# GpSimd makes the low half of every seventh weight chunk of the experts

## The chip, the cores and the metric

One core of one Trainium2 chip runs the whole program. The metric is the device time of one execution in microseconds (us). Three runs of the kernel before took 1637.53, 1638.44 and 1640.66 us; the median is 1638.44 us. A profiled execution is a run of its own; all positions below (such as 1096.76) are microseconds from the start of its span.

## The reference, cut to what matters

The model has two layers over 256 tokens of width 1024. The last part of the second layer is a mixture of experts, and this part holds all that the change touches:

```python
def moe_swiglu(x, router, w_gate, w_up, w_down):
    logits = (x @ router).astype(jnp.float32)
    top_vals, top_idx = lax.top_k(logits, TOP_K)          # TOP_K = 2 of N_EXPERTS = 8
    gates = jax.nn.softmax(top_vals, axis=-1)
    combine = jnp.sum(jax.nn.one_hot(top_idx, N_EXPERTS) * gates[..., None], axis=-2)
    y = jnp.zeros_like(x)
    for e in range(N_EXPERTS):
        y = y + combine[..., e:e + 1] * swiglu(x, w_gate[e], w_up[e], w_down[e])
    return y
```

`swiglu` is `(silu(x @ w_gate) * (x @ w_up)) @ w_down`. Per expert `w_gate` and `w_up` are 1024 x 3584 and `w_down` is 3584 x 1024, all float32.

## The kernel before, in words

**Chunks.** All weights stream from HBM in chunks of 128 partitions x 2048 float32 (1 MB). The even and odd layers take 98 chunks (`N0`), each expert 42 (`EC`): 28 for gate and up (four per 512 hidden columns: gate, gate, up, up) and 14 for down. SyncE issues the DMAs in chunk order into a ring of raw buffers, six before the experts and seven in them (`NEXP = 7`; `raw_exp[n % 7]`).

**High and low halves.** A float32 product is made of three products in the type `float32r`. For each chunk ScalarE writes the high half, `w_hi = raw` rounded (a copy, line 1116 in the profile, semaphore `hi_made`). Then VectorE writes the low half, `w_lo = raw - w_hi` (`w_split`, line 1964 in the experts; `split`, line 1483, before them; semaphore `lo_made`). TensorE waits for `lo_made` and runs 12 matmuls per chunk of the experts: for each of 4 rows of weights hi x hi (line 397), hi x lo (398), lo x hi (399). At the end it counts up `chunk_used`.

**Buffers.** There are three pairs of `w_hi`/`w_lo` and, in the experts, a fourth pair `w_hi_more`/`w_lo_more`. The table `E_SLOT` gives each chunk of an expert its pair, in cycles of 4, 4, 4, 4, 4, 3, 3, 4, 4, 4, 4 chunks (`E_CYCLES`). So most chunks use the pair that was used four chunks before, and the chunks 23 to 28 the one used three chunks before. ScalarE can write `w_hi` of a chunk only when that earlier chunk is used.

**One expert.** Each engine runs the same list of 42 steps per expert, in an order written out by hand (`expert(job, z)` on TensorE, ScalarE and VectorE). The first seven experts are a loop, the eighth (`z`) is written out with extra work. At step c VectorE makes the low halves of `E_SPLIT[c]`, that is of chunk c + 4 or c + 3. Besides: at step 0 it makes two `pick` tiles for the next expert (`picks`, line 1855), which TensorE reads in the `index` matmuls (line 793) just before chunk 4 (`C_INDEX = 4`). At steps 3, 7, 11, ... it makes `e_h`, the hidden activations (line 1957), which TensorE transposes (line 864) after chunks 5, 9, 13, ... . `eT_lo` (line 1973) is the low half of these transposed activations.

**GpSimd.** It makes masks, and five low halves before the experts (`split`, line 1010, same subtraction). In the loop over the experts it only issues one indirect DMA per expert (`get_x`, line 1077), which gathers the rows of the next expert. In the eighth expert it issues the gathers of the results of the others (`get_y`, line 1086), each after VectorE has added the one before (`add_got`, line 1932, semaphore `y_added`). In that expert VectorE also computes the row numbers (lines 1890 to 1910) and the gate weights (lines 1915 to 1926).

**What else waits for the low halves.** SyncE issues the DMA of chunk c when the low half of chunk c - 7 is made, since that frees the raw buffer.

Of the kernel before, what the change touches and what calls it, by code (L numbers as in the profile page):

```python
# [18 lines left out]
F32 = mybir.dt.float32  # L19
# [3 lines left out]
ALU = mybir.AluOpType  # L23
# [8 lines left out]
def trunk(nc, x, mem, ln_g, ln_b, mem_wq, mem_wkv, mem_wo, ab_w_in, ab_sinks, ab_w_out,  # L32
# [4 lines left out]
    TB = SEQ // P  # L37
# [11 lines left out]
    W = 512  # L49
# [61 lines left out]
    with ExitStack() as ctx:  # L111
# [172 lines left out]
        for n in range(NSPL + 1, EC + NSPL + 1):  # L284
            at_step = max(at_step, max(m for m in range(-EC, n) if E_SLOT[m % EC] == E_SLOT[n % EC]))
            E_SPLIT[at_step].append(n)
        C_GOT = {12 + 4 * n: (n // TB, n % TB) for n in range(2 * TB)}
# [77 lines left out]
        def _(pe):  # L365
            pair = [0]

            def chunk_product(c, outs, lhs_hi, lhs_lo, k0, first, last, cols, idx=None, slot=None,
                              rows=None, done=None, ready=None, turned=False):
# [3 lines left out]
                pe.wait_ge(lo_made, c + 1 if idx is None else idx + 1)  # L373
# [449 lines left out]
            def expert(job, z):  # L823
                start = list(claims)
                for c in range(EC):
# [14 lines left out]
                    if c < 4 * EJ:  # L840
                        j, q = c // 4, c % 4
                        key, b = (f"{z}eg{j}", j % 2) if q < 2 else (f"{z}eu{j}", 2 + j % 2)
                        if q % 2 == 0:
                            claim(pe, key, b, job, signal=False)
                        chunk_product(c, [(0, bank[b])], xe_hi, xe_lo, 4 * (q % 2), q % 2 == 0,
                                      q % 2 == 1, W, idx=idx, slot=E_SLOT[c], done=chunk_used)
                    else:
# [3 lines left out]
                        if i == 0:  # L851
# [4 lines left out]
                                      done=chunk_used)  # L856
# [29 lines left out]
        def _(sp):  # L886
# [14 lines left out]
            def expert_chunks(e, job, first=False):  # L901
                for c in range(EC):

                    if first and c < NRAW:
                        sp.wait_ge(lo_made, N0 + c - NRAW + 1)
                    elif first and c == NRAW:

                        wait_filled(sp, "router0")
                    else:
                        sp.wait_ge(lo_made, N0 + c - NEXP + 1 + EC * job)  # L910
# [31 lines left out]
        def _(pool):  # L942
# [153 lines left out]
            last = pool.value_load(last_job[0:1, 0:1], min_val=NE - 1, max_val=2 * NE - 1)  # L1096
            with pool.Fori(0, last) as job:
                pool.wait_ge(sem("index_made"), job + 1)
                pool.sem_inc(sem("x_asked"), 1)
                get_x()  # L1100
            for half in range(2):

                pool.wait_ge(sem(f"y_kept{half}"), 16 * last + 16)
                pool.sem_inc(sem("y_asked"), 1)
            pool.wait_ge(sem("rows_made"), 1)
            for g in range(2 * TB):
                get_y(g)

# [345 lines left out]
        def _(dve):  # L1454
# [492 lines left out]
            def expert(job, z):  # L1947
                for c in range(EC):
# [12 lines left out]
                    def w_split(n, job=job):  # L1961
                        r, s = n % NEXP, E_SLOT[n % EC]
                        dve.wait_ge(hi_made, N0 + n + 1 + EC * job)
                        tt(w_lo[s][:, :], raw_exp[r][:, :], w_hi[s][:, :].bitcast(F32),  # L1964
                           ALU.subtract).then_inc(lo_made, 1)
# [89 lines left out]
```

## Time and profile before

| what | value |
|---|---|
| median of three runs | 1638.44 us |
| span of the profiled execution | 1639.8 us |
| TensorE matmul busy | 1599.7 us (98%) |
| VectorE busy | 1259.6 us (77%) |
| ScalarE busy | 1029.8 us (63%) |
| GpSimd busy | 121.1 us (7%) |
| mean granted clock of TensorE | 0.991 |

The page gives the span of the profiled execution from its first to its last instruction and no time of its own beside it. The span is 1.4 us above the median of the three runs. A digit row of the page (one digit for each fortieth of the span, 9 for 90% or more) has TensorE at 9 nearly everywhere, VectorE at 8 or 9 in the last 60%, where the experts are, and the DMA engines at 9 there. In a group of instructions the columns are: line, engine, operation, what it writes and reads, shapes, count, busy time in all, mean duration in ns, and then how long the engine was idle just before these instructions and what ended that.

### The profile page before, as it was taken

The numbers are of one execution on the slowest core, as the hardware profiler recorded it, in microseconds if no ns is written. First come the engines' busy times: TensorE is split into PE (matmuls) and PEld (weight loads), VectorE is DVE, ScalarE is ACT, GpSimd is POOL, SyncE is SP. The second block draws the span as 40 slices with busy tenths as digits, with TensorE's granted clock in tenths as the row PEclk, the third lists the DMA queues.
The fourth block names the chain that finished last, engine by engine and source line by source line (L and its number), as shares of the span: only waits on it lengthen the run. The fifth ranks groups of instructions, "written<-read, shape, count | busy, mean of one in ns | idle before, by whom it ended". The sixth has DMA issues, their size and how long they took to land.

```text
span 1639.8 us, 22497 instructions
## 1 busy us (share of the span) xinstructions
PE 1599.7 (98%) x8202; PEld 1347.1 (82%) x8202; DVE 1259.6 (77%) x1173; ACT 1029.8 (63%) x920; POOL 121.1 (7%) x131
## 2 busy tenths in 40 slices
PE   9999999999999998999999999999999999999996
PEld 8888988888896796888888888888888888888775
DVE  4687475554647656889889889888988988988996
ACT  4564444343437454677777777777777777777673
POOL 2103010000104101000000000000000000000120
PEclk9999999999999999999999999999999999999999
DMA  9437656466455363899999999999999999999992
GB/s 351 164 127 252 213 182 216 128 219 200 161 193 185 135 206 105 318 364 377 389 363 385 389 364 375 389 371 384 388 368 387 388 358 386 388 362 389 359 369 94
DMA packets 238397, 481.24 MB, mean 293 GB/s; under 512 B 8256, under 2 KB 11360, under 8 KB 238336
## 3 DMA queue, kind: packets, MB, share of 16 engines
q1 hardware_dynamic: 229744, 454.06, 77.3%
q0 software_dynamic: 6576, 22.68, 4.1%
q10 hardware_dynamic: 2016, 3.67, 0.6%
q8 instruction: 40, 0.66, 0.2%
q14 instruction: 21, 0.17, 0.0%
HBM read 474.07 MB, written 11.56 MB: 296 GB/s over the span
## 4 chain that ended last, share of the span: by engine, by line
PE 84%; DVE 9%; issue 2%; DMA 2%; ACT 2%; POOL 1%; POOLq 0%; DVEq 0%; SPq 0%; ACTq 0%
PE bank L397 23%; PE bank L399 23%; PE bank L398 23%; PE bank L387 3%; PE bank L390 3%; PE bank L389 3%; DVE w_lo L1483 2%; PE bank L864 1%; DVE w_lo L1964 1%; DMA y_got<-y_rows,row_i 1%; PE bank L684 1%; PE bank L660 1%; DVE X L1520 1%; ACT w_hi L1116 1%; DVE X L1529 1%
## 5 line engine op out<-in xcount | busy, mean ns | idle before, releaser
L1116 ACT ACTIVATE w_hi<-raw 128x2048 fp32r<-128x2048 f32 (+1 forms) x322 | 608.8, 1895 | 258.7 <-PE bank L399 220.3
L1964 DVE TENSOR_TENSOR w_lo<-raw,w_hi 128x2048 fp32r<-128x2048 f32 x221 | 503.1, 2290 | 81.8 <-ACT w_hi L1116 78.5
L1483 DVE TENSOR_TENSOR w_lo<-raw,w_hi 128x2048 fp32r<-128x2048 f32 (+1 forms) x96 | 211.2, 2204 | 145.5 <-ACT w_hi L1116 145.2
L397 PE MATMUL bank<-w_hi,xe_hi 128*128 128x512 f32 x736 | 292.9, 398 | 1.2 <-DVE w_lo L1964 1.2
L399 PE MATMUL bank<-w_hi,xe_lo 128*128 128x512 f32 x736 | 287.9, 391 | 0.0
L398 PE MATMUL bank<-w_lo,xe_hi 128*128 128x512 f32 x736 | 287.4, 390 | 0.0
L399 PEld LDWEIGHTS bank<-w_hi,xe_lo 128*128 128x128 f32 x736 | 138.5, 188 | 29.9
L397 PEld LDWEIGHTS bank<-w_hi,xe_hi 128*128 128x128 f32 x736 | 138.6, 188 | 28.8 <-DVE w_lo L1964 1.6
L398 PEld LDWEIGHTS bank<-w_lo,xe_hi 128*128 128x128 f32 x736 | 138.8, 189 | 27.4
L1964 DVE TENSOR_TENSOR w_lo_more<-raw,w_hi_more 128x2048 fp32r<-128x2048 f32 x63 | 144.2, 2290 | 18.5 <-ACT w_hi_more L1116 11.4
L397 PE MATMUL bank<-w_hi,xT_hi 128*128 128x512 f32 (+1 forms) x384 | 147.0, 383 | 0.1
L399 PE MATMUL bank<-w_hi,xT_lo 128*128 128x512 f32 (+1 forms) x384 | 144.5, 376 | 0.0
L398 PE MATMUL bank<-w_lo,xT_hi 128*128 128x512 f32 (+1 forms) x384 | 144.5, 376 | 0.0
L1116 ACT ACTIVATE w_hi_more<-raw 128x2048 fp32r<-128x2048 f32 x64 | 122.9, 1920 | 28.0 <-PE bank L399 23.8
L397 PE MATMUL bank<-w_hi,eT_hi 128*128 128x512 f32 x320 | 125.8, 393 | 0.5 <-DVE w_lo L1964 0.5
L399 PE MATMUL bank<-w_hi,eT_lo 128*128 128x512 f32 x320 | 124.6, 390 | 0.0
L398 PE MATMUL bank<-w_lo,eT_hi 128*128 128x512 f32 x320 | 124.6, 389 | 0.0
L387 PE MATMUL bank<-xT_hi,w_hi 128*128 128x256 f32 x352 | 101.1, 287 | 2.1 <-DVE w_lo L1483 2.1
L389 PE MATMUL bank<-xT_lo,w_hi 128*128 128x256 f32 x352 | 100.3, 285 | 0.0
L390 PE MATMUL bank<-xT_hi,w_lo 128*128 128x256 f32 x352 | 100.3, 285 | 0.0
L1964 DVE TENSOR_TENSOR w_lo<-raw_more,w_hi 128x2048 fp32r<-128x2048 f32 x40 | 91.4, 2286 | 3.7 <-ACT w_hi L1116 3.7
L1116 ACT ACTIVATE w_hi<-raw_more 128x2048 fp32r<-128x2048 f32 x40 | 76.7, 1916 | 25.0 <-PE bank L399 25.0
(291 smaller groups left out, 2598.4 us busy)
## 6 DMA issues: line engine op xcount, KB each, us to landing
raw<-in_moe_w_gate_dram SPq DMA_DIRECT2D x96, 1024.0 KB, 9.2
raw<-in_moe_w_up_dram SPq DMA_DIRECT2D x96, 1024.0 KB, 8.4
raw<-in_moe_w_down_dram SPq DMA_DIRECT2D x96, 1024.0 KB, 7.2
raw<-in_mem_wkv_dram SPq DMA_DIRECT2D x16, 1024.0 KB, 5.1
raw_more<-in_moe_w_up_dram SPq DMA_DIRECT2D x16, 1024.0 KB, 8.7
raw_more<-in_moe_w_gate_dram SPq DMA_DIRECT2D x16, 1024.0 KB, 8.7
raw_more<-in_moe_w_down_dram SPq DMA_DIRECT2D x16, 1024.0 KB, 7.8
raw<-in_c_w_in_dram SPq DMA_DIRECT2D x12, 1024.0 KB, 5.2
```

Source lines behind the costliest of these rows:

```text
L387: nc.tensor.matmul(d, wh, xh, start=(first and k == 0 and q % 2 == 0), stop=False, skip_group_check=True)
L389: nc.tensor.matmul(d, wh, xl, start=False, stop=False, skip_group_check=True)
L390: m = nc.tensor.matmul(d, wl, xh, start=False, stop=(last and k == n - 1), skip_group_check=True)
L397: nc.tensor.matmul(d, xh, hi[:, k, :], start=(first and k == 0), stop=False)
L398: nc.tensor.matmul(d, xh, lo[:, k, :], start=False, stop=False)
L399: m = nc.tensor.matmul(d, xl, hi[:, k, :], start=False, stop=(last and k == n - 1))
L660: m = nc.tensor.matmul(d[:, t * SEQ:(t + 1) * SEQ], QK[:, 2 * h + k, t * P:(t + 1) * P], MK[:, 2 * h + k, :], start=(k == 0), stop=(k == 1))
L684: m = nc.tensor.matmul(d[:, k * SEQ:(k + 1) * SEQ], MV[:, mb, c:c + P], PT_t[i % 2][:, mb * SEQ:(mb + 1) * SEQ], start=(mb == 0), stop=(mb ...
L864: m = nc.tensor.transpose(d[:, q * P:(q + 1) * P], e_h[j % 2][:, q * P:(q + 1) * P], ident[:, :])
L1116: return nc.scalar.activation(dst, src, ACT.Copy)
L1483: tt(w_lo[s][:, 0:n], raw[c % NRAW][:, 0:n], w_hi[s][:, 0:n].bitcast(F32), ALU.subtract).then_inc(lo_made, 1)
L1964: tt(w_lo[s][:, :], raw_exp[r][:, :], w_hi[s][:, :].bitcast(F32), ALU.subtract).then_inc(lo_made, 1)
```

## The change

Of the 42 chunks of an expert, the six with n % 7 == 5 after the first four, that is 5, 12, 19, 26, 33 and 40, get their low half from GpSimd and not from VectorE. They all lie in the same raw buffer. GpSimd counts them on a semaphore of its own, `lo_by_pool`. `split_done(c, job)` says which semaphore and which value stand for chunk c; TensorE and SyncE wait by it. VectorE leaves these six out. In the loop GpSimd makes chunk 5 ahead of `get_x` and the others behind it. In the eighth expert it makes chunk 5 first, then 12 behind the first pair of gathers, 19 behind the second, and 26, 33 and 40 behind the fourth.

```diff
+        POOL_SPLITS = [n for n in range(NSPL + 1, EC) if n % NEXP == NEXP - 2]
+        DVE_EC = EC - len(POOL_SPLITS)
+
+        def split_done(c, job):
+
+            if c < 0:
+                return split_done(c + EC, job - 1)
+            before_c = sum(n < c for n in POOL_SPLITS)
+            if c in POOL_SPLITS:
+                return sem("lo_by_pool"), before_c + 1 + len(POOL_SPLITS) * job
+            return lo_made, N0 + c + 1 - before_c + DVE_EC * job
...
-                pe.wait_ge(lo_made, c + 1 if idx is None else idx + 1)
+                pe.wait_ge(*((lo_made, c + 1) if idx is None else split_done(c, job)))
...
-                        sp.wait_ge(lo_made, N0 + c - NEXP + 1 + EC * job)
+                        sp.wait_ge(*split_done(c - NEXP, job))
...
+            def w_split(n, job):
+
+                r, s = n % NEXP, E_SLOT[n % EC]
+                pool.wait_ge(hi_made, N0 + n + 1 + EC * job)
+                nc.gpsimd.tensor_tensor(w_lo[s][:, :], raw_exp[r][:, :], w_hi[s][:, :].bitcast(F32),
+                                        ALU.subtract).then_inc(sem("lo_by_pool"), 1)
+
             with pool.Fori(0, last) as job:
+                w_split(POOL_SPLITS[0], job)
                 pool.wait_ge(sem("index_made"), job + 1)
                 pool.sem_inc(sem("x_asked"), 1)
                 get_x()
+                for n in POOL_SPLITS[1:]:
+                    w_split(n, job)
+            w_split(POOL_SPLITS[0], last)
...
+            late_splits = {0: POOL_SPLITS[1:2], 1: POOL_SPLITS[2:3], 2 * TB - 1: POOL_SPLITS[3:]}
             for g in range(2 * TB):
                 get_y(g)
+                for n in late_splits.get(g, ()):
+                    w_split(n, last)
...
                     def w_split(n, job=job):
                         r, s = n % NEXP, E_SLOT[n % EC]
+                        if n in POOL_SPLITS:
+                            return
```

GpSimd's loop over the first seven experts, in the kernel before (`x_got` are the gathered rows, the branch closes the loop):

```order
L1097 UNCONDITIONAL_BRANCH
L1097 ISA
L1077 DMA x_got<-x_rows,got_i 128x1024
L1097 REGISTER_ALU
L1097 COMPARE_AND_BRANCH
L1103 ISA
```

The same loop in the changed kernel (`w_lo_...` and `w_hi_...` are the pairs of buffers, `raw_50` is the one raw buffer of these six chunks):

```order
L1113 TENSOR_TENSOR w_lo_58<-raw_50,w_hi_55 128x2048
L1118 REGISTER_ALU
L1089 DMA x_got<-x_rows,got_i 128x1024
L1112 REGISTER_ALU
L1113 TENSOR_TENSOR w_lo_60<-raw_50,w_hi_57 128x2048
L1112 REGISTER_ALU
L1113 TENSOR_TENSOR w_lo_more<-raw_50,w_hi_more 128x2048
L1112 REGISTER_ALU
L1113 TENSOR_TENSOR w_lo_60<-raw_50,w_hi_57 128x2048
L1112 REGISTER_ALU
L1113 TENSOR_TENSOR w_lo_more<-raw_50,w_hi_more 128x2048
L1112 REGISTER_ALU
```

The loop had one instruction that moves data; now six subtractions stand beside it, one ahead of the gather and five behind. The sixth, of chunk 40, follows the last row shown.

VectorE around the start of an expert (here the eighth, the loop has the same pattern), in the kernel before. The first row is the low half of chunk 4, `w_lo_58<-raw_50` is that of chunk 5, and `raw_more` belongs to chunk 6:

```order
L1964 TENSOR_TENSOR w_lo_60<-raw_49,w_hi_57 128x2048
L1855 ISA
L1855 TENSOR_SCALAR pick<-slot_no,place 128x128
L1855 ISA
L1855 TENSOR_SCALAR pick<-slot_no,place 128x128
L1963 REGISTER_ALU
L1964 TENSOR_TENSOR w_lo_58<-raw_50,w_hi_55 128x2048
L1963 REGISTER_ALU
L1964 TENSOR_TENSOR w_lo_59<-raw_more,w_hi_56 128x2048
```

The same place in the changed kernel:

```order
L1992 TENSOR_TENSOR w_lo_60<-raw_49,w_hi_57 128x2048
L1881 ISA
L1881 TENSOR_SCALAR pick<-slot_no,place 128x128
L1881 ISA
L1881 TENSOR_SCALAR pick<-slot_no,place 128x128
L1991 REGISTER_ALU
L1992 TENSOR_TENSOR w_lo_59<-raw_more,w_hi_56 128x2048
```

The low half of chunk 5 is gone from behind the two picks, and that of chunk 6 moves up. The picks and all ahead of them stay where they were.

## Rows read from the trace of the kernel before

**Rows 1.** Page, part 1: busy time, share of the span, instructions of each engine

```profile
PE 1599.7 (98%) x8202; PEld 1347.1 (82%) x8202; DVE 1259.6 (77%) x1173; ACT 1029.8 (63%) x920; POOL 121.1 (7%) x131
```

**Rows 2.** Windows: first, fourth and eighth expert; length, busy by engine, clock, DMA

```profile
665.60:784.70 119.10, 119.10 (x545) 98.72 (x545) 105.84 (x63) 90.28 (x61) 2.67 (x1) 1.00 1.00 363
1022.80:1141.80 119.00, 119.00 (x546) 98.61 (x545) 104.75 (x62) 90.18 (x61) 2.67 (x1) 1.00 1.04 381
1498.80:1625.50 126.70, 122.60 (x539) 98.85 (x538) 111.33 (x96) 83.52 (x57) 18.09 (x8) 0.99 0.85 313
```

**Rows 3.** Groups of ScalarE in the fourth expert, the costliest

```profile
L1116 ACT ACTIVATE w_hi<-raw 128x2048 fp32r<-128x2048 f32 x28 | 53.6, 1917 | 14.7 <-PE bank L399 14.0 <-ACT y L1116 0.7
```

**Rows 4.** Line 1010: ns min/median/max; timeline around one (start, duration, instruction, idle before)

```profile
L1010 POOL TENSOR_TENSOR w_lo<-raw,w_hi x5: 4607/4612/4617, 136.6 to 634.3; 128x2048 fp32r<-128x2048 f32 x5
...
410.31 1.92 ACT L1116 ACTIVATE w_hi<-raw 128x2048 fp32r<-128x2048 f32 x1 [4.38 <-PE bank L399]
...
412.40 4.61 POOL L1010 TENSOR_TENSOR w_lo<-raw,w_hi 128x2048 fp32r<-128x2048 f32 x1 [174.61 <-ACT w_hi L1116]
```

**Rows 5.** Timeline of the fourth expert around chunk 26

```profile
1091.16 1.92 ACT L1116 ACTIVATE w_hi<-raw 128x2048 fp32r<-128x2048 f32 x1 [0.32 <-PE bank L399]
...
1094.11 2.29 DVE L1964 TENSOR_TENSOR w_lo<-raw,w_hi 128x2048 fp32r<-128x2048 f32 x1 [0.22 <-DVE e_h L1957]
...
1096.41 0.60 PE L864 MATMUL bank<-ident,e_h 128*128 128x128 f32 x4
1096.76 0.48 PE L397 MATMUL bank<-w_hi,xe_hi 128*128 128x512 f32 x1
```

**Rows 6.** Timeline of the fourth expert around chunk 40

```profile
1128.38 1.92 ACT L1116 ACTIVATE w_hi<-raw 128x2048 fp32r<-128x2048 f32 x1 [0.35 <-PE bank L399]
...
1136.34 0.39 PE L397 MATMUL bank<-w_hi,eT_hi 128*128 128x512 f32 x1
```

**Rows 7.** Line 1520: ns min/median/max of its instructions; timeline, the longest of them

```profile
L1520 DVE SCALAR_TENSOR_TENSOR X<-X,mean_var,gb x10: 1265/1266/1801, 142.0 to 644.7; 128x1024 f32<-128x1024 f32 x10
...
416.29 1.80 DVE L1520 SCALAR_TENSOR_TENSOR X<-X,mean_var,gb 128x1024 f32<-128x1024 f32 x1
```

**Rows 8.** Line 1662: ns min/median/max; timeline of one beside GpSimd's

```profile
L1662 DVE TENSOR_SCALAR neg_max<-row_max,neg_sinks x8: 228/574/576, 62.9 to 85.4; 128x2 f32<-128x2 f32 x8
...
62.88 0.57 DVE L1662 TENSOR_SCALAR neg_max<-row_max,neg_sinks 128x2 f32<-128x2 f32 x1
...
62.92 2.33 POOL L1002 TENSOR_SCALAR a_add<-dist 128x384 f32<-128x384 f32 x2 [21.83 <-DVE row_max L1656]
```

**Rows 9.** Timeline of the fourth expert around the picks and chunk 5

```profile
1029.68 1.91 ACT L1116 ACTIVATE w_hi<-raw 128x2048 fp32r<-128x2048 f32 x1
...
1031.75 0.28 DVE L1855 TENSOR_SCALAR pick<-slot_no,place 128x128 f32<-128x128 f32 x1
...
1033.64 0.50 PE L793 MATMUL bank<-token_no,pick 128*128 128x1 f32 x4
...
1036.87 0.39 PE L397 MATMUL bank<-w_hi,xe_hi 128*128 128x512 f32 x1
```

**Rows 10.** Timeline of the first expert: high half of chunk 5, the two picks, the index

```profile
671.84 1.91 ACT L1116 ACTIVATE w_hi<-raw 128x2048 fp32r<-128x2048 f32 x1
...
673.66 0.47 DVE L1855 TENSOR_SCALAR pick<-slot_no,place 128x128 f32<-128x128 f32 x2
...
676.59 0.50 PE L793 MATMUL bank<-token_no,pick 128*128 128x1 f32 x4
```

**Rows 11.** Eighth expert: TensorE's waits; its timeline; three windows

```profile
PE bank L397 <- DVE w_lo L1964: 1.7, 2, 1.2
...
1529.46 0.65 PE L864 MATMUL bank<-ident,e_h 128*128 128x128 f32 x4 [2.08 <-DVE e_h L1957]
...
1530.70:1534.00 3.30, 3.30 (x9) 2.54 (x8) 3.30 (x3) 0.00 (x0) 0.00 (x0) 0.50 0.66 196
1571.00:1574.00 3.00, 1.79 (x9) 1.27 (x8) 3.00 (x2) 1.91 (x1) 2.69 (x2) 1.00 0.64 220
```

More of the change, by code:

```diff
@@ L368, in chunk_product @@
             def chunk_product(c, outs, lhs_hi, lhs_lo, k0, first, last, cols, idx=None, slot=None,
-                              rows=None, done=None, ready=None, turned=False):
+                              rows=None, done=None, ready=None, turned=False, job=None):
                 n = chunks[c][1] if idx is None else CK
-                pe.wait_ge(lo_made, c + 1 if idx is None else idx + 1)
+                pe.wait_ge(*((lo_made, c + 1) if idx is None else split_done(c, job)))
                 s = c % NSPL if slot is None else slot
@@ L845, in expert @@
                         chunk_product(c, [(0, bank[b])], xe_hi, xe_lo, 4 * (q % 2), q % 2 == 0,
-                                      q % 2 == 1, W, idx=idx, slot=E_SLOT[c], done=chunk_used)
+                                      q % 2 == 1, W, idx=idx, slot=E_SLOT[c], done=chunk_used, job=job)
                     else:
@@ L855, in expert @@
                                       q == EK // CK - 1, W, idx=idx, slot=E_SLOT[c],
-                                      done=chunk_used)
+                                      done=chunk_used, job=job)
                     if c % 4 == 1 and 1 <= c // 4 <= EJ:
```

## The prediction

> **What bounds the kernel now.** I read the page's first part, then the windows of single experts, then the groups of ScalarE, then the timeline chunk by chunk. TensorE is busy for 98% of the span [rows 1]. In the first and the fourth expert it is busy for the whole window, 119.1 of 119.10 us and 119.0 of 119.00, at full granted clock, while VectorE has 105.84 and 104.75 us of work [rows 2]. So in the experts of the loop TensorE never waits, and VectorE is free for 13 to 14 us of each. ScalarE's idle time before the high halves was ended by TensorE (14.0 of 14.7 us), none of it by a DMA [rows 3]: the weights are there before they are wanted. Only the eighth expert has slack on TensorE: 126.70 us long, 122.60 busy, with VectorE at 111.33 [rows 2]. Its waits are for VectorE: 2.08 us ahead of the transposes at 1529.46, followed by a stretch of 3.3 us at a granted clock of 0.50 (the lower level, 1.2 GHz), and 1.7 us in two waits for low halves, the longest 1.2 us, after which the clock stayed at 1.00 [rows 11].
>
> This decides what relief of VectorE can bring. In seven experts it brings nothing. In the eighth it can give back at most 2.08, plus what the low clock cost (half of 3.3, so 1.7 us), plus 1.7: 5.5 us. What matters more is whether a low half from GpSimd comes in time.
>
> **Removed.** Six subtractions of 2.29 us per expert leave VectorE, 13.7 us per expert. TensorE covers all of that in the loop.
>
> **Added: the longer subtraction.** GpSimd needs 4.61 us for the same shape, in all five cases between 4607 and 4617 ns, and starts 0.17 us after the high half ends (410.31 + 1.92 = 412.23, start 412.40) [rows 4]. A low half is then ready 4.78 us after its high half. For chunk 5 of the fourth expert the high half ends at 1031.59, the low half would be ready at 1036.37, and TensorE starts the chunk at 1036.87 [rows 9]: in time by 0.5 us. For chunk 40: 1130.30 + 4.78 = 1135.08 against 1136.34 [rows 6]: in time by 1.3 us. Chunks 12, 19 and 33 have a pair four chunks old as 5 and 40 have, and I take them as in time too. Chunk 26 is the exception. Its pair is the one used three chunks before, so its high half comes late: 1091.16 + 1.92 = 1093.08. The low half is ready at 1097.86, and TensorE starts the chunk at 1096.76, right behind the transposes at 1096.41 [rows 5]. TensorE waits 1.1 us, and since it is the bound, nothing later gives this back. Eight experts: 8.8 us. VectorE had that low half ready at 1094.11 + 2.29 = 1096.40, which is why nothing of this is seen now.
>
> **Added: two engines that want the same reads.** The one place where a long subtraction of GpSimd and a VectorE instruction with two inputs in SBUF overlap is at 416.29. That instruction took 1.80 us; its nine like took 1265 or 1266 ns, so it was held for 0.536 us [rows 7], until 416.83, which is 4.43 us after GpSimd's start at 412.40 [rows 4]. I read this as: while GpSimd subtracts, such an instruction of VectorE stands still. A held low half in the loop costs VectorE up to 4.43 - 2.29 = 2.14 us net per moved chunk. Its work would be 104.75 + 6 x 2.14 = 117.6 us of 119.0: just under TensorE's pace, so in the loop I price this at 0.
>
> It is not free where TensorE waits for a short instruction of VectorE. Look at the start of an expert. The high half of chunk 5 ends at 1031.59, GpSimd would start at 1031.76, and the second `pick` starts at 1031.75 and takes 0.28 us [rows 9]. These two now meet. Who goes first? The nearest case is `neg_max`, an instruction with SBUF inputs on VectorE of two elements per partition. It starts at 62.88, GpSimd's instruction at 62.92, and it takes 0.57 us where the shortest of its kind took 228 ns [rows 8]. So VectorE's instruction was held though its record began 0.04 us sooner. The second pick leads by only 0.01 us, and I take it as held until 1031.76 + 4.43 = 1036.19; it ends at 1036.47. Behind it on VectorE wait the low halves of chunks 6 and 7 and `e_h`, which have room. TensorE wants the picks in the index matmuls at 1033.64 [rows 9], ahead of chunk 4, and would start them 2.8 us late. A wait of 2.08 us was followed by a low clock that cost 1.7 us, one of 1.2 us was not [rows 11]. Whether every wait of 2.8 us is, no row tells; bounds 0 and 1.7, I take 1.1.
>
> The Trainium skill, page "SBUF — State Buffer", section "Who interferes with whom", says that a Vector instruction with two SBUF inputs contends with a GpSimd instruction that reads SBUF, and that "Issue order, not op shape, decides who blocks". The row at 416.29 agrees on the hold (0.536 us, to near GpSimd's end); the `neg_max` row, where the later record won, does not follow the order of the records. Taken strictly, the rule lets the pick go first, and the index then waits for nothing: this is the first rival below.
>
> In the first expert the high half ends at 673.75, GpSimd starts at 673.92, and the second pick starts at 673.66 + 0.47 - 0.28 = 673.85 [rows 10], 0.07 us ahead. That is more than the 0.04 of the held case, so I take 0 there; held, it costs 673.92 + 4.43 + 0.28 - 676.59 = 2.0 us.
>
> **The eighth expert.** The pick is held as in the loop (2.8), chunk 26 is late (1.1). VectorE is late there anyway, so held instructions reach TensorE. At least the waits for chunks 4 and 26 remain (3.9); at most all five other holds show in full, 3.9 + 5 x 2.14 = 14.6. I take two of them, at chunk 5 (ahead of the row numbers and `e_h`) and at chunk 19 (ahead of `add_got`, whose end releases the next gather): 3.9 + 4.3 = 8.2. The gain of 5.5 us is then not had.
>
> **SyncE.** The DMA of chunk c + 7 is issued when a moved low half is done, up to 2.4 us later. No high half waited for a DMA [rows 3]; I price it at 0, and the cover is gone only if the buffers run empty.
>
> **Sum.** Experts 2 to 7: 6 x (1.1 + 2.8 + 1.1) = 30.0. First: 1.1. Eighth: 8.2. Together 39.3, on the profiled execution's 1639.8 gives 1679.1. The median of the runs lies 1.4 lower: **1677.7 us**. Low end of this case: no clock cost, eighth at 3.9: 6 x 3.9 + 1.1 + 3.9 = 28.4, so 1666.8. High end: 6 x 5.6 + (1.1 + 2.0 + 1.7) + 14.6 + 1.7 = 54.7, so 1693.1.
>
> **Rivals.**
> - The pick goes first. For it: it leads by 0.01 us, and it comes straight behind another pick with no wait between. Against it: the held case above. Then 8 x 1.1 plus 4.3 in the eighth expert = 13.1, so 1651.5 (1647 to 1663).
> - No holding that matters. For it: only one row shows a hold by this subtraction. Then 8.8 less what the eighth expert gives back, of at most 5.5 say 4: +4.8, so 1643.2.
> - Faster: VectorE's relief in the eighth expert pays and chunk 26 does not wait. It decides at 1096.76 - 1093.08 - 0.17 = 3.5 us: if GpSimd's subtraction took less than that beside full engines, the whole 5.5 came back, 1632.9. All five rows say 4.61.
> - Worse: held low halves push VectorE past TensorE's pace, since 117.6 of 119.0 leaves 1.4 us. At 3 us more per expert that is 8 x 3 on top: about 1702.
>
> **How the numbers follow.** Forecast 0.55, pick first 0.28, no holding 0.09, faster 0.03, worse 0.05. The range 1647 to 1694 leaves out the last three and holds both likelier cases. A measurement here can tell about 0.2% (3.3 us) from no change. Faster by more: 0.03. Within: 0.05, from the third case when more than 4 us come back. Slower: 0.92.
>
> **What would show it.** In the loop TensorE waits for GpSimd's `w_lo` 1.1 us at chunk 26 in every expert, and ahead of the index matmuls 2.8 us with a `pick` of about 4.7 us on VectorE. Experts 2 to 7 take 123 to 125 us and not 119. VectorE's `w_lo` has durations between 2.3 and 6.7 us. The forecast is wrong if picks stay at 0.28 us (first rival), if all `w_lo` stay at 2.29 us (second), or if GpSimd's subtraction is itself longer than 4.7 us beside VectorE's back-to-back work, as it then makes more than one chunk late.

## The result: 3.1% slower, and the profile after

The changed kernel takes 1688.97 us (median of 4 runs, 1680.85 to 1699.53) against 1637.99 us before (4 runs, 1636.16 to 1640.66): a ratio of 1.0314, with a 95% interval of 1.0273 to 1.0355. The forecast was 1677.7, with a range of 1647 to 1694. The profiled execution after took 1690.17 us with a span of 1688.4, which is 48.6 us more than the span before.

Page of the kernel after, part 1 (busy time, share of the span, instructions), which answers to [rows 1]:

```profile
PE 1613.7 (96%) x8202; PEld 1353.1 (80%) x8202; DVE 1267.0 (75%) x1125; ACT 1031.1 (61%) x920; POOL 356.5 (21%) x179
```

VectorE has 48 instructions fewer and is busy for 7.4 us *more*. 48 low halves of 2.29 us left it, 110 us; other instructions have grown by a little more than that.

Windows tell where the time went. First the seven experts of the loop as one stretch, in the kernel before, counted from the end of chunk 2 of the first expert to the end of chunk 2 of the eighth (columns: length, busy time by engine TensorE, weight load, VectorE, ScalarE, GpSimd, granted clock, DMA share, GB/s):

```profile
674.04:1507.18 833.14, 833.14 (x3809) 690.41 (x3809) 732.76 (x426) 630.94 (x427) 18.68 (x7) 1.00 1.03 378
```

In the kernel after: the same stretch, then the first and the fourth expert, the eighth up to its last chunk (these three answer to [rows 2]), and three short stretches of low clock:

```profile
671.09:1540.91 869.82, 846.27 (x3809) 697.21 (x3809) 734.45 (x384) 632.23 (x427) 225.56 (x49) 0.99 1.00 362
...
662.65:784.85 122.20, 119.51 (x545) 98.58 (x545) 105.52 (x56) 90.47 (x61) 32.27 (x7) 1.00 0.97 349
1034.15:1158.75 124.60, 121.13 (x545) 99.73 (x544) 105.03 (x56) 90.39 (x61) 32.27 (x7) 0.99 1.00 362
...
1532.50:1674.10 141.60, 126.15 (x540) 100.76 (x538) 117.38 (x91) 83.46 (x56) 45.79 (x14) 0.96 0.79 282
...
1049.70:1053.10 3.40, 3.40 (x10) 2.71 (x9) 3.15 (x3) 0.48 (x1) 0.00 (x0) 0.52 1.05 387
1569.00:1575.80 6.80, 6.17 (x17) 5.04 (x18) 5.00 (x3) 0.02 (x1) 0.00 (x0) 0.52 0.40 118
1616.20:1619.60 3.40, 3.33 (x8) 2.66 (x9) 3.40 (x4) 0.00 (x0) 3.07 (x3) 0.53 0.63 175
```

The reader should see three things. The loop became 36.7 us longer (869.82 - 833.14): 23.6 us of it TensorE's idle time, which was nought before, and 13.1 us more busy time with the same 3809 matmuls. Most of that second part is the clock: each of the experts 2 to 7 has one stretch of 3.4 us at half clock, which costs 1.7 us, so 10.2 us. The 2.9 us left are some 0.2 us behind each of 14 waits, called TensorE's restart here. A version below in which the clock stays at 1.00 shows it alone: two waits in an expert, and 119.50 us busy in place of 119.02. In the eighth expert the same work took 141.6 us in place of 126.7. And VectorE's busy time per expert did not move: 105.03 us for 56 instructions, where [rows 2] have 104.75 for 62.

What TensorE waited for, in the whole kernel after (line 805 is the `index`, 876 the transposes of `e_h`, 409 the first matmul of a row of weights, 848 the transposes of `pick` in the eighth expert; columns: us in all, times, longest), which answers to the first row of [rows 11]:

```profile
PE bank L805 <- DVE pick L1881: 17.9, 7, 2.7
PE bank L876 <- DVE e_h L1983: 6.5, 2, 6.1
PE bank L409 <- DVE w_lo L1992: 6.2, 3, 2.9
PE bank L409 <- POOL w_lo L1113: 5.6, 7, 0.8
...
PE bank L848 <- DVE pick L1881: 2.7, 1, 2.7
```

Seven waits for a `pick` and seven for GpSimd's low half make 17.9 + 5.6 = 23.5 us: all of the loop's idle time. None of the 17.9 us is a wait for a result that GpSimd makes.

Timeline of the kernel after around the picks of the fourth expert (start, duration, instruction, idle time before it in brackets), the same place as [rows 9]:

```profile
1041.11 1.91 ACT L1142 ACTIVATE w_hi<-raw 128x2048 fp32r<-128x2048 f32 x1
...
1042.98 4.78 DVE L1881 TENSOR_SCALAR pick<-slot_no,place 128x128 f32<-128x128 f32 x2
...
1043.10 4.58 POOL L1113 TENSOR_TENSOR w_lo<-raw,w_hi 128x2048 fp32r<-128x2048 f32 x1 [15.44 <-ACT w_hi L1142]
...
1047.68 2.28 DVE L1992 TENSOR_TENSOR w_lo<-raw_more,w_hi 128x2048 fp32r<-128x2048 f32 x1
...
1047.89 0.60 PE L805 MATMUL bank<-token_no,pick 128*128 128x1 f32 x4 [2.66 <-DVE pick L1881]
```

The high half ends at 1043.02, GpSimd starts at 1043.10. Of the two picks one took 278 ns and the other 4585 ns: the second ends at 1047.76, right behind GpSimd's end at 1047.68. GpSimd itself needs 4.58 us, no more than alone. So the two did not share: GpSimd ran at its own speed, and the pick stood still.

Timeline of the kernel after around chunk 26 of the fourth expert, the same place as [rows 5]:

```profile
1107.09 1.92 ACT L1142 ACTIVATE w_hi<-raw 128x2048 fp32r<-128x2048 f32 x1 [0.31 <-PE bank L411]
...
1109.09 4.60 POOL L1113 TENSOR_TENSOR w_lo<-raw,w_hi 128x2048 fp32r<-128x2048 f32 x1 [18.11 <-ACT w_hi L1142]
1109.14 0.68 DVE L1983 TENSOR_TENSOR e_h<-bank,e_g 128x512 f32<-128x512 f32 x1
...
1111.76 4.08 DVE L1992 TENSOR_TENSOR w_lo<-raw_more,w_hi 128x2048 fp32r<-128x2048 f32 x1 [1.95 <-ACT w_hi L1142]
...
1113.75 0.50 PE L409 MATMUL bank<-w_hi,xe_hi 128*128 128x512 f32 x1 [0.81 <-POOL w_lo L1113]
```

GpSimd ends at 1113.69, and TensorE starts chunk 26 at 1113.75 after 0.81 us of idleness. VectorE's next low half takes 4.08 us in place of 2.29, as it is held until GpSimd is done, and nobody waits for it. `e_h`, of whose two inputs one (`bank`) lies in PSUM, started 0.05 us behind GpSimd and took its usual 0.68 us: it is not held.

Timeline of the kernel after in the eighth expert, where GpSimd makes the low half of chunk 12:

```profile
1562.79 0.23 DVE L1948 TENSOR_TENSOR g<-g,w_fin 128x2 f32<-128x2 f32 x2
1562.88 4.53 POOL L1113 TENSOR_TENSOR w_lo<-raw,w_hi 128x2048 fp32r<-128x2048 f32 x1 [8.00 <-ACT w_hi L1142]
1562.94 4.50 DVE L1949 TENSOR_TENSOR w_fin<-w_fin 128x2 f32<-128x2 f32 x1
...
1567.46 1.23 DVE L1952 TENSOR_SCALAR X<-X 128x2048 f32<-128x2048 f32 x1
1568.81 0.69 DVE L1983 TENSOR_TENSOR e_h<-bank,e_g 128x512 f32<-128x512 f32 x1
1569.63 1.11 PE L876 MATMUL bank<-ident,e_h 128*128 128x128 f32 x4 [6.07 <-DVE e_h L1983]
```

`w_fin` has two elements per partition. It took 4.50 us. Behind it stand `X` and `e_h`, and TensorE waits 6.07 us for `e_h`.

### The profile page after: what moved, and what is told of

Its sections match the earlier page's. It is cut to its first block, busy times and chain, and to the rows that moved or that the text cites. A ratio compares the mean times of both kernels' runs of the same rounds, so it can differ in the third digit from the quotient of the medians.

```text
span 1688.4 us, 22505 instructions
## 1 busy us (share of the span) xinstructions
PE 1613.7 (96%) x8202; PEld 1353.1 (80%) x8202; DVE 1267.0 (75%) x1125; ACT 1031.1 (61%) x920; POOL 356.5 (21%) x179
## 4 chain that ended last, share of the span: by engine, by line
PE 51%; issue 22%; DVE 12%; POOL 8%; ACT 4%; DMA 3%; ACTq 0%; DVEq 0%; POOLq 0%; SPq 0%
PE bank L409 14%; PE bank L410 13%; PE bank L411 13%; POOL w_lo L1113 4%; ACT w_hi L1142 2%; DVE pick L1881 2%; PE bank L399 2%; PE bank L402 2%; PE bank L401 2%; POOL w_lo_more L1113 2%; DMA c_add<-gate_rows 2%; DVE w_lo L1509 2%; DVE w_lo L1992 1%; POOL x_got L1089 1%; PE bank L696 1%
## 5 line engine op out<-in xcount | busy, mean ns | idle before, releaser
L1992 DVE TENSOR_TENSOR w_lo<-raw,w_hi 128x2048 fp32r<-128x2048 f32 x189 | 431.2, 2307 | 56.1 <-ACT w_hi L1142 52.8
L409 PE MATMUL bank<-w_hi,xe_hi 128*128 128x512 f32 x736 | 298.0, 405 | 8.5 <-POOL w_lo L1113 5.6
L410 PE MATMUL bank<-w_lo,xe_hi 128*128 128x512 f32 x736 | 292.0, 397 | 0.0
L411 PE MATMUL bank<-w_hi,xe_lo 128*128 128x512 f32 x736 | 291.7, 396 | 0.0
L1113 POOL TENSOR_TENSOR w_lo<-raw,w_hi 128x2048 fp32r<-128x2048 f32 x32 | 151.9, 4747 | 402.9 <-ACT w_hi L1142 402.9
L1992 DVE TENSOR_TENSOR w_lo<-raw_more,w_hi 128x2048 fp32r<-128x2048 f32 x40 | 149.8, 3744 | 62.2 <-ACT w_hi L1142 62.2
L1113 POOL TENSOR_TENSOR w_lo_more<-raw,w_hi_more 128x2048 fp32r<-128x2048 f32 x16 | 82.8, 5175 | 212.0 <-ACT w_hi_more L1142 212.0
L410 PE MATMUL bank<-w_lo,eT_hi 128*128 128x512 f32 x320 | 124.6, 389 | 0.0
L1992 DVE TENSOR_TENSOR w_lo_more<-raw,w_hi_more 128x2048 fp32r<-128x2048 f32 x47 | 107.5, 2287 | 13.4 <-ACT w_hi_more L1142 8.1
```

The costliest lines, as they stand in the source:

```text
L409: nc.tensor.matmul(d, xh, hi[:, k, :], start=(first and k == 0), stop=False)
L410: nc.tensor.matmul(d, xh, lo[:, k, :], start=False, stop=False)
L411: m = nc.tensor.matmul(d, xl, hi[:, k, :], start=False, stop=(last and k == n - 1))
L1113: nc.gpsimd.tensor_tensor(w_lo[s][:, :], raw_exp[r][:, :], w_hi[s][:, :].bitcast(F32), ALU.subtract).then_inc(sem("lo_by_pool"), 1)
```

## The experiments

My theory was: the loss is made by two low halves per expert, 5 (it holds a `pick`) and 26 (it is late itself), by the clock behind the wait for the pick, and by holds in the eighth expert. The rival was that the hold matters little or falls differently, and that GpSimd's slowness as such is the cause. For every kernel the spans of single experts are read from TensorE's count of used chunks, from the end of chunk 2 to the end of chunk 2 of the next expert. Before, that is 119.02 us in each, and the rest from chunk 2 of the eighth on, called the tail here, is 132.59 us. After it is 122.2, then 124.6 six times, and a tail of 147.5.

**Without chunk 26.** GpSimd makes 5, 12, 19, 33 and 40, VectorE 26.

```diff
-        POOL_SPLITS = [n for n in range(NSPL + 1, EC) if n % NEXP == NEXP - 2]
+        POOL_SPLITS = [5, 12, 19, 33, 40]
```

> The changed kernel, but chunk 26 goes back to VectorE (GpSimd keeps 5, 12, 19, 33, 40). Theory: TensorE waits for GpSimd's low half at chunk 26 alone, 1.1 us per expert, and the wait at the index is another thing. So experts 2 to 7 take 124.6 - 1.1 = 123.5 us each, no TensorE wait for a low half of GpSimd is left in the loop, and the time falls by about 9 us, to 1680. Rival (the waits come from VectorE being held in general, so that moving one chunk only shifts them): the wait appears at another chunk and the length of an expert stays within 0.3 us of 124.6.

Measured: 1680.92 us (1679.61 to 1681.46), ratio 1.0259 (1.0242 to 1.0276). Experts 2 to 7 take 123.5 us, two of them 125.0; the waits for the pick are there unchanged (17.9 us, 7 times), those for GpSimd's low half in the loop are gone. So chunk 26 costs 1.1 us per expert (124.6 - 123.5). In the two long experts the low clock lasted 6.8 us and not 3.4. The total came out as expected, but not by the expected sum of eight times 1.1: the loop gave back 4.6 us and the tail 4.8 (142.7 in place of 147.5), for a reason that is read below with the eighth expert.

**Without chunk 5.** GpSimd makes 12, 19, 26, 33 and 40.

```diff
-        POOL_SPLITS = [n for n in range(NSPL + 1, EC) if n % NEXP == NEXP - 2]
+        POOL_SPLITS = [12, 19, 26, 33, 40]
```

> The changed kernel, but chunk 5 goes back to VectorE. Theory: the index wait of 2.7 us and the low clock behind it come from GpSimd's subtraction of chunk 5 alone. So the second pick takes 0.28 us again, experts 2 to 7 take 119.0 + 1.1 = 120.1 us, the clock stays at 1.00 in them, and the time is 1650 to 1660. Rival (the load on VectorE as a whole does it): the index wait stays above 1 us and an expert above 122 us.

Measured: 1660.2 us (1657.91 to 1662.74), ratio 1.0129 (1.0112 to 1.0146). Each expert of the loop takes 120.1 us, that is 1.07 over before, all of it at chunk 26, and there is no low clock in the loop. Line 1887 (the picks) in one expert of this kernel (min, median and max in ns):

```profile
L1887 DVE TENSOR_SCALAR pick<-slot_no,place x2: 279/279/279, 1035.5 to 1035.7; 128x128 f32<-128x128 f32 x2
```

The one low half of chunk 5 thus cost 124.6 - 120.1 = 4.5 us per expert, four times what chunk 26 costs, though it is itself never late. The tail was still 145.6 us: chunk 5 is not what makes most of the eighth expert's loss.

**The picks ahead of GpSimd.** The changed kernel, but GpSimd starts on chunk 5 only when the picks are made. It still does all its work.

```diff
                 r, s = n % NEXP, E_SLOT[n % EC]
+                if n == 5:
+                    pool.wait_ge(sem("picked"), job + 2)
                 pool.wait_ge(hi_made, N0 + n + 1 + EC * job)
```

> The changed kernel with all six chunks on GpSimd, but GpSimd waits for the two picks of the same step before it starts chunk 5. Theory (the pick and the subtraction collide): the subtraction starts about 0.4 us later, its low half is ready just before TensorE wants it, the index wait goes, and experts 2 to 7 take 120.1 to 120.5 us; 1650 to 1660 in all. Rival (chunk 5 is too slow on GpSimd wherever it starts, and the wait only shows at the index): TensorE waits at chunk 5 instead and an expert stays above 122 us.

Measured: 1661.14 us (1658.05 to 1663.4), ratio 1.0136 (1.0118 to 1.0153). Timeline of this kernel at the same place of the fourth expert:

```profile
1035.66 0.48 DVE L1883 TENSOR_SCALAR pick<-slot_no,place 128x128 f32<-128x128 f32 x2
1036.32 4.61 POOL L1115 TENSOR_TENSOR w_lo<-raw,w_hi 128x2048 fp32r<-128x2048 f32 x1 [15.90 <-DVE pick L1883]
1037.55 5.53 DVE L1994 TENSOR_TENSOR w_lo<-raw_more,w_hi 128x2048 fp32r<-128x2048 f32 x1 [1.40 <-ACT w_hi L1144]
1037.75 0.50 PE L805 MATMUL bank<-token_no,pick 128*128 128x1 f32 x4
```

Starting GpSimd *later* makes the kernel 28 us faster. Both picks are at 0.28 us, the index waits for nothing, and the clock stays at 1.00. The hold has only moved to the next instruction (5.53 us for a low half), which has room in the loop. This is the plainest evidence that the 17.9 us are a hold and no want of VectorE time: VectorE has more held time here (106.3 us busy per expert) than after. An expert takes 120.76 us: 1.05 for chunk 26 and 0.7 more at chunks 5, 12 and 14, on which more below.

**VectorE makes all low halves of the eighth expert.** The loop is as in the changed kernel.

```diff
-                        if n in POOL_SPLITS:
+                        if n in POOL_SPLITS and not z:
                             return
```

> The changed kernel, but in the eighth expert VectorE makes all low halves; the first seven are as in the changed kernel. Theory: the eighth expert and what follows lost 14.9 us, so the time falls by about 15 us, to 1674, and experts 2 to 7 stay at 124.6 us. Rival (part of the eighth expert's loss is carried over from the loop, by buffers that come free late): it falls by less than 8 us.

Measured: 1666.81 us (1664.48 to 1681.57), ratio 1.0202 (1.0152 to 1.0252). The tail is 133.6 us, 1.0 over before: of the eighth expert's loss of 14.9 us, 13.9 are due to its own low halves on GpSimd, and 1.0 stays open. The loop held a surprise. Window of the fourth expert of this kernel, and the index in it:

```profile
1038.48:1161.45 122.97, 119.50 (x545) 98.58 (x545) 105.06 (x56) 90.38 (x62) 32.26 (x7) 1.00 1.00 366
```
```profile
1043.85 0.60 PE L805 MATMUL bank<-token_no,pick 128*128 128x1 f32 x4 [2.67 <-DVE pick L1878]
```

The wait is the same 2.67 us, yet the granted clock is 1.00. Only in the second expert of this execution did the clock fall; the third to the seventh take 122.97 us and not 124.6, and the first 120.06, as its pick was not held (on which more in the next section). So a wait of 2.7 us costs 0 or 1.7 us by way of the clock, on the same code. One of the four runs of this kernel took 1681.57 us and the three others 1664.5 to 1667.9, and there is no trace of it. Its mean granted clock is on record: 0.985, against 0.992 in the profiled execution. By an estimate, (1 - clock) x span is the time lost to the clock: 25.2 and 13.3 us, so 11.9 of the 15.8 us between these two lie there, about seven stretches of 3.4 us more. Where they lay is not known.

**All three at once.** Without 26, picks first, eighth expert by VectorE.

```diff
+        POOL_SPLITS = [5, 12, 19, 33, 40]
...
+                if n == 5:
+                    pool.wait_ge(sem("picked"), job + 2)
...
+                        if n in POOL_SPLITS and not z:
```

> GpSimd makes five low halves (5, 12, 19, 33, 40) in each of the first seven experts, starts chunk 5 behind the picks, and VectorE makes chunk 26 and all of the eighth expert. Theory: all three causes are gone, TensorE waits for nothing in the loop, and the time is that of the kernel before, 1638 within 4 us. VectorE is still held 2 us or more at each moved chunk, without a cost. Rival (contention costs something everywhere): experts 2 to 7 stay more than 0.5 us above 119.0 each, 1642 or more in all.

Measured: 1643.37 us (1642.01 to 1644.53), ratio 1.0031 (1.0018 to 1.0043). Nearly all is given back: the tail is 132.8 us, an expert 119.70. The 0.7 us left per expert lie at chunks 5, 12 and 14, as with the picks ahead of GpSimd (0.12, 0.43 and 0.12 us). The timeline of this kernel shows the cause of the largest, at chunk 12 of the fourth expert:

```profile
1049.71 2.29 DVE L1995 TENSOR_TENSOR w_lo_more<-raw,w_hi_more 128x2048 fp32r<-128x2048 f32 x1 [0.22 <-ACT w_hi L1145]
1049.79 6.70 POOL L1115 TENSOR_TENSOR w_lo<-raw,w_hi 128x2048 fp32r<-128x2048 f32 x1 [0.67 <-ACT w_hi L1145]
...
1053.03 5.61 DVE L1995 TENSOR_TENSOR w_lo<-raw_more,w_hi 128x2048 fp32r<-128x2048 f32 x1 [1.03 <-ACT w_hi L1145]
```

Here VectorE's low half of chunk 11 started 0.08 us ahead and ran in its 2.29 us. Now GpSimd is the one that is held: 6.70 = 4.61 + 2.09, where 2.09 lies just under the 2.21 us that VectorE still had to go. So the hold works both ways, and its price is what remains of the neighbour's time. In the same trace VectorE's chunk 13 then stands behind GpSimd (5.61 us).

**The four that should be free.** The changed kernel with GpSimd making chunks 12, 19, 33 and 40 in the loop, neither 5 nor 26, and the eighth expert by VectorE.

```diff
-        POOL_SPLITS = [n for n in range(NSPL + 1, EC) if n % NEXP == NEXP - 2]
+        POOL_SPLITS = [12, 19, 33, 40]
...
-                        if n in POOL_SPLITS:
+                        if n in POOL_SPLITS and not z:
```

> The changed kernel with GpSimd making chunks 12, 19, 33 and 40 in the loop's experts, neither 5 (beside the picks) nor 26 (behind an outlier of the transfers), and VectorE all of the eighth expert. Theory (only those two splits and the eighth expert cost anything; the four others are hidden although each holds a neighbour by about 2 us): 119.0 to 119.1 us per expert of the loop, 132.6 to 133 us for the eighth and end, 1637 to 1640 us. Rival (chunk 12's 0.4 us in the last version of this kind is there with or without a low half of chunk 5 by GpSimd): 119.4 us per expert, 1641 us. Rival (work taken off VectorE brings something once nothing is in its way): under 1636 us.

Measured: 1638.21 us (10 runs, 1635.63 to 1640.91) against 1638.96 (19 runs), ratio 0.9995 (0.9985 to 1.0005). An expert takes 119.02 us, no chunk differs from before by 0.1 us in the fourth expert, and the tail is 133.1 us. Window of the fourth expert, and VectorE's groups in the fourth and fifth:

```profile
1027.22:1146.24 119.02, 119.02 (x545) 98.64 (x545) 104.11 (x58) 90.19 (x62) 23.83 (x5) 1.00 1.04 381
```
```profile
L1990 DVE TENSOR_TENSOR w_lo<-raw_more,w_hi 128x2048 fp32r<-128x2048 f32 x10 | 35.6, 3564 | 11.9 <-ACT w_hi L1140 11.9
...
L1990 DVE TENSOR_TENSOR w_lo_more<-raw_more,w_hi_more 128x2048 fp32r<-128x2048 f32 x2 | 9.5, 4765 | 3.8 <-ACT w_hi_more L1140 3.8
```

Four low halves per expert have left VectorE, 9.2 us, and its busy time fell from 104.75 [rows 2] to 104.1: the low half behind each moved one is held. These are among the rows that read `raw_more`, with means of 3.56 and 4.77 us in place of 2.29, though in the first row the chunks 6 and 27 (four of ten) follow no moved one. Moving this work brings VectorE 0.65 us of the 9.2, and would bring the kernel nothing if it brought more, as TensorE is busy for 119.02 of 119.02 us. The chunk 12 loss is gone together with chunk 5 on GpSimd.

**A read that makes nothing.** The kernel before, in which VectorE makes every low half; GpSimd only subtracts two tiles of 1024 numbers at the high halves of four chunks, and the difference is not used.

```diff
+            def beside(k, n, job):
+                pool.wait_ge(sem("spare_made"), k + 1 + 4 * job)
+                pool.wait_ge(hi_made, N0 + n + 1 + EC * job)
+                nc.gpsimd.tensor_tensor(spare[:, :], gb[:, 0, :], gb[:, 1, :], ALU.subtract)\
+                    .then_inc(sem("spare_made"), 1)
...
             with pool.Fori(0, last) as job:
+                beside(0, 5, job)
...
                 get_x()
+                beside(1, 12, job)
+                beside(2, 19, job)
+                beside(3, 33, job)
```

> The kernel before, in which VectorE makes every low half, with one more GpSimd instruction in each expert of the loop at the large part of chunks 5, 12, 19 and 33: a difference of two tiles of 1024 numbers that nothing uses, written where nothing is kept. Theory (GpSimd's two-tile read holds VectorE, or is held by it, whatever the result is for): the extra instruction is about 2.3 us long alone (half of 4.6); at chunk 5 a pick beside it takes about 2.3 us in place of 0.28, the index transposes wait 0 to 0.5 us more; at 12, 19 and 33 either VectorE's low half is about 2.1 us longer (4.0 in place of 1.9) or the extra instruction is about 2 us longer (4.3). VectorE's low halves are then late by up to 2.1 us of the about 2.7 us that TensorE leaves: 119.0 to 119.7 us per expert, 1638 to 1643 us in all. Rival (the loss of the changed kernel comes only from GpSimd's slower making of the low half, with no hold): all VectorE times as before, picks 0.28 us, 1638 us.

Measured: 1642.77 us (10 runs, 1639.72 to 1643.74) against 1638.96, ratio 1.0018 (1.0009 to 1.0028). Timeline of this kernel in the fourth expert, at chunk 5 and then at chunk 12:

```profile
1028.59 2.62 DVE L1869 TENSOR_SCALAR pick<-slot_no,place 128x128 f32<-128x128 f32 x2
1028.72 2.41 POOL L1102 TENSOR_TENSOR spare<-gb 128x1024 f32<-128x1024 f32 x1 [36.70 <-ACT w_hi L1130]
...
1031.35 0.60 PE L793 MATMUL bank<-token_no,pick 128*128 128x1 f32 x4 [0.50 <-DVE pick L1869]
...
1047.14 2.29 DVE L1978 TENSOR_TENSOR w_lo_more<-raw,w_hi_more 128x2048 fp32r<-128x2048 f32 x1 [0.22 <-DVE e_h L1971]
1048.19 3.51 POOL L1102 TENSOR_TENSOR spare<-gb 128x1024 f32<-128x1024 f32 x1 [1.65 <-ACT w_hi L1130]
1049.35 4.51 DVE L1978 TENSOR_TENSOR w_lo<-raw,w_hi 128x2048 fp32r<-128x2048 f32 x1
```

Nothing waits for this instruction, and yet the experts 2 to 7 take 0.73 us more each, at the index. The hold of the pick scales with GpSimd's instruction: 2.41 us of GpSimd give a pick of 2.43 us, 4.58 gave 4.59. The rival, that only GpSimd's slow low half costs time, falls with this kernel. So does another, that a hold needs a buffer that both engines use: GpSimd reads `gb` here, the pick `slot_no` and `place`. Whether it is GpSimd's reading or its writing that holds VectorE, no version here separates; `e_h`, which writes SBUF as a low half does but reads one input from PSUM, was not held. In the second group the two take turns: GpSimd, started in the middle of VectorE's instruction, waits for its end (3.51 = 2.41 + 1.10; VectorE had 1.24 us to go), then VectorE's next, back to back, waits for GpSimd's end (4.51 = 2.28 + 2.23). I had expected one or the other, and got both. But they do not always take turns. Timeline of this kernel in the first expert:

```profile
669.39 6.93 POOL L1102 TENSOR_TENSOR spare<-gb 128x1024 f32<-128x1024 f32 x1 [22.88 <-ACT w_hi L1130]
...
669.58 2.29 DVE L1978 TENSOR_TENSOR w_lo<-raw,w_hi 128x2048 fp32r<-128x2048 f32 x1
...
671.78 2.28 DVE L1978 TENSOR_TENSOR w_lo<-raw_more,w_hi 128x2048 fp32r<-128x2048 f32 x1
```

Here GpSimd, started while a pick of 0.28 us ran, stood until VectorE had made two low halves more (6.93 = 2.41 + 4.52), and this first expert took 119.01 us, as before. What decides between the two, no run here tells.

**The eighth expert apart.** Two versions of the changed kernel whose loop is unchanged. In the eighth expert GpSimd makes only chunk 12:

```diff
-                        if n in POOL_SPLITS:
+                        if n in POOL_SPLITS and (not z or n in [12]):
```

> The changed kernel, of whose GpSimd low halves in the eighth expert only chunk 12 is left (VectorE makes 5, 19, 26, 33 and 40 there). Theory (chunk 12's low half holds the gate weights, on which the first output tile and its bank depend, and so TensorE waits some 6 us): from chunk 2 of the eighth expert to the end 139 to 141 us, against 133.6 where VectorE makes all and 147.5 where GpSimd makes all six; 1668 to 1684 us in all, by how often the clock falls in the loop. Rival (the loss comes from the index transposes and the later splits): 134 to 135 us there.

Measured: one run of 1683.66 us; tail 136.8 us. The other version gives chunk 12 to VectorE and leaves the other five (`n in [5, 19, 26, 33, 40]`):

> The changed kernel, in whose eighth expert VectorE makes chunk 12 and GpSimd the other five. Theory: from chunk 2 of the eighth expert to the end 140 to 143 us (3.9 for the index and chunk 5, 1.1 for chunk 26, the rest from later holds and the clock), so chunk 12 alone is worth 5 to 7 of the 147.5; 1670 to 1686 us in all. Rival (chunk 12 is worth nothing beside the others): 147 us.

Measured: one run of 1689.76 us; tail 144.8 us. So chunk 12 costs 4.2 us alone (136.8 - 132.6; 3.2 by the 133.6 of the version in which VectorE makes all there) and the five others 12.2. Together they cost 14.9, so chunk 12 on top of the others adds only 2.7. Both of my sizes were off: I had given chunk 12 at least 6.4 us and the five at most 10.4. The cause at chunk 12 is as the timeline of after showed it: TensorE waits 6.4 us for `e_h` there, in place of 2.1 before. What TensorE waited for in the tail of the version without it:

```profile
PE bank L409 <- DVE w_lo L1993: 6.7, 4, 3.0
PE bank L848 <- DVE pick L1882: 2.7, 1, 2.7
...
PE bank L876 <- DVE e_h L1984: 0.7, 2, 0.5
```

The five cost by a pick held for 2.7 us and by VectorE being late with its *own* low halves (6.7 us, before 1.7). This execution has three stretches of low clock within the tail's chunks, of 3.4, 3.4 and 6.8 us; before has one of 3.4.

How much chunk 12 costs hangs on when its high half is made. Timeline of the version without chunk 26 in the eighth expert, where `X`, the last of the gate weights' steps, ends at 1559.89:

```profile
1559.87 4.61 POOL L1113 TENSOR_TENSOR w_lo<-raw,w_hi 128x2048 fp32r<-128x2048 f32 x1 [9.45 <-ACT w_hi L1148]
...
1560.01 0.69 DVE L1989 TENSOR_TENSOR e_h<-bank,e_g 128x512 f32<-128x512 f32 x1
```

GpSimd came after the gate weights' steps there, held none of them, and TensorE's waits for `e_h` in the tail are 0.6 us in all in place of 6.5. In that execution the clock had fallen once before this place in the tail, and TensorE's chunks and the high halves behind them came later. By the waits (5.9 us less for `e_h`, 2.4 more for the low half behind it) this shift of 1.4 us is worth 3.5 of the 4.8 us that the version gave back in its tail. The tail of the version with the picks ahead of GpSimd is short as well, 142.4 us, and its waits for `e_h` are 3.2 us.

**Gate weights later.** The kernel before, with the gate weights two chunks later, to see whether the 2.08 us of [rows 11] can be had without GpSimd.

```diff
-                    if z and c == 6:
+                    if z and c == 8:
                         gate_weights()
```

> The kernel before, but in the eighth expert VectorE computes the gate weights at step 8 and not at step 6, behind the hidden activations that TensorE waited 2.08 us for. Theory: the wait and the low clock behind it (1.7 us) go: 1634 to 1636, a gain of 2 to 4 us. Rival (the next sum of VectorE becomes late by as much): no change.

Measured: 1639.68 us (11 runs) against 1637.88 (17 runs), ratio 1.0007 (0.9996 to 1.0019): no change. The one long wait for `e_h` and the low clock behind it are gone (four waits remain, 1.6 us in all, the longest 0.5), but TensorE's waits for low halves grew from 1.7 to 3.1 us, and the tail is 132.95 us. The slack of the eighth expert was turned into another wait. No version here beats the kernel before.

## Why the prediction was right, and where its sizes were off

By its steps:

- **What bounds the kernel.** Right. TensorE is the bound in the loop (833.14 of 833.14 us), and relief of VectorE brings nothing: the version with the four harmless low halves is at 0.9995 of before.
- **The longer subtraction.** 4.61 us taken, 4.58 and 4.60 found. The start was taken as 0.17 us behind the high half, and is 0.07 to 0.08. Chunk 26: 1.1 us forecast, 1.07 measured without chunk 5. Chunks 12, 19, 33 and 40 in time: right for the changed kernel, though its GpSimd is held for up to 1.3 us there (5.88 us at chunk 33), which I had not priced.
- **The held pick.** Right in what came: 2.8 us forecast, 2.66 waited, 2.89 with TensorE's restart where the clock stayed up. The step that led there was not right, and that the forecast case came was luck. I had the pick lead by 0.01 us and took it as held, by the likeness of `neg_max`. With the start at 0.08 us it was GpSimd that led, by 0.08 us (1047.76 - 4.585 = 1043.18 against 1043.10). Where a pick did lead by 0.01 us, it was not held. It happened in the first expert of two versions; this is the one with the eighth expert on VectorE:

```profile
670.64 0.28 DVE L1878 TENSOR_SCALAR pick<-slot_no,place 128x128 f32<-128x128 f32 x1
670.65 4.75 POOL L1113 TENSOR_TENSOR w_lo<-raw,w_hi 128x2048 fp32r<-128x2048 f32 x1 [24.05 <-ACT w_hi L1139]
```

  GpSimd waited instead (4.75 in place of 4.58 us). So by these two cases, with the start that the prediction took, its first rival would have come true. The Trainium skill, page "SBUF — State Buffer", section "Who interferes with whom", says that issue order decides who blocks. The trace agrees in these cases: the pick that starts 0.08 us after GpSimd's read is held 4.3 us, GpSimd starting 0.08 us after VectorE's read is held 2.09 us, and the pick that leads by 0.01 us is free. That the rule would save the pick was my reading of a start that was 0.09 us off. `neg_max`, held in all five cases in which it led by 0.05 us, stays unexplained. **In the first expert** I took 0 for a pick that would lead by 0.07 us. Both records start at 670.88, the pick took 4.67 us, and TensorE waited 1.9 us.
- **The clock.** 1.1 us per expert was taken between the bounds 0 and 1.7. In the profiled execution all six experts had the full 1.7; in the version with the eighth expert on VectorE one in six had it. Both ends are real, and the upper one is not the last: two experts of the version without chunk 26 had 6.8 us of low clock. For this execution the term is 0.6 us per expert too low, 3.6 in all.
- **VectorE's load in the loop.** The 117.6 us was a bound: a full hold of 4.43 us for each moved chunk, less the 2.29 us taken off. Measured are 105.03. In the fourth expert the holds come to 14.2 us, 4.3 for the pick and 1.6 to 2.6 for each of five low halves, against 13.7 us taken off. No low half there was held in full, since each starts 2.7 to 3.2 us behind GpSimd. The price of 0 for this step was right, and the rival "worse" did not come.
- **The eighth expert.** This is the term that was mis-sized: 8.2 us forecast, 14.9 measured. "I take two of them, at chunk 5 and at chunk 19" failed. The hold that counted most in one place was at chunk 12, on `w_fin`, one of the steps of the gate weights, which I had not laid beside GpSimd's start. The price of 2.14 us was wrong for it too. That price takes off the low half that VectorE no longer makes, but the one of chunk 12 stands behind `e_h` in VectorE's list (at 1531.77 before, `e_h` at 1528.64), so the whole hold of 4.3 us (4.50 less the 0.15 that `w_fin` took before) fell on `e_h`. Even the bound of 14.6 was passed. The parts by the profile of after: 2.7 for the pick, 4.2 more for `e_h` (6.5 - 2.3), 4.5 more for low halves (6.2 - 1.7), and 3.4 for 6.8 us more at half clock: 14.8.
- **SyncE at nought.** Right. ScalarE's idle time before its high halves in the fourth expert was ended by TensorE for 19.0 of 19.7 us and by no DMA.

The median lies 11.3 us above the forecast (1688.97 - 1677.7). The sum against the spans: 39.3 forecast, 48.6 measured. First expert 3.2 (1.1 forecast), experts 2 to 7 33.5 (30.0), tail 14.9 (8.2), and the part before the experts 3.0 *less*. That last is scatter: this part, which no version changes, took between 669.6 and 674.7 us in the executions here.

Of the expected signs, the picks are at 4.6 us, the experts 2 to 7 at 124.6 us in the 123 to 125 forecast, and the low halves of VectorE between 2.3 and 6.7 us.

## What to carry to other kernels

Work that is moved to GpSimd is not off VectorE when both read two inputs from SBUF, as the low halves do: one of the two stands while the other runs. A short instruction such as a pick is held just as long. So lay each long GpSimd instruction beside VectorE's list, look for the short instructions that the bound engine waits for, and put GpSimd behind them (worth 28 us here). Where the bound engine is busy for the whole stretch, the best that relief of another can reach is no change, as the version with four low halves shows.

## What the runs showed of the hardware that I had not expected

- The hold goes both ways. GpSimd's 4.61 us became 6.70 behind VectorE, and in the kernel with the useless read GpSimd waited 1.10 us for VectorE, and VectorE's next instruction then 2.23 us for GpSimd. In its first expert GpSimd waited 4.52 us, for a pick and two low halves in a row.
- A hold is paid by size of the neighbour, not of the held one: a `w_fin` of 128x2 took 4.50 us.
- The same wait of 2.7 us on TensorE was followed by a low clock in each of the experts 2 to 7 of three executions (after, without chunk 26, and chunk 12 alone in the eighth), in five of the six of a fourth, and in one of six of another. The spread of whole runs grows with it: the changed kernel's four runs lie 18.7 us apart, with mean clocks of 0.989 in the fastest and 0.979 in the slowest. By the estimate of (1 - clock) x span that is 18.5 and 35.7 us lost, so 17.2 of the 18.7 us are the clock. The harmless version's six runs lie 2.5 us apart.
- What reads one of its two inputs from PSUM was not held: `e_h` took 0.68 us in the midst of GpSimd's 4.60 us, and the 56 of them in the changed kernel's experts have a mean of 677 ns.
